# Fourier position transform with its 512-column moving operand turned afterwards, and query latents normed and turned ahead of it

## What is computed

```python
h = rmsnorm(x, ln_mix_g)
z = jnp.einsum('bsd,dn->bsn', h, w_in)
c_q, c_kv, k_rope, u = z[..., :o1], z[..., o1:o2], z[..., o2:o3], z[..., o3:]
y_mix = jnp.concatenate([mla(c_q, c_kv, k_rope, q_norm_g, w_uq, kv_norm_g, w_ukv),
                         fourier_mix(u, w_fnet)], axis=-1)
x = x + jnp.einsum('bsn,nd->bsd', y_mix, w_out)
...
def fourier_mix(u, w_fnet):
    B, S, _ = u.shape
    ug = u.reshape(B, S, FNET_GROUPS, FNET_GROUP_DIM).astype(jnp.float32)
    f = jnp.fft.fftn(ug, axes=(1, 3), norm='ortho').real.astype(u.dtype)
    return jnp.einsum('bsgc,gcd->bsgd', f, w_fnet).reshape(B, S, FNET_WIDTH)
```

## Time and profile before

| | us |
|---|---|
| median of 3 runs (lowest to highest) | 1427.01 (1426.34 to 1427.31) |
| the profiled execution | 1423.45 |
| its span, first to last instruction | 1421.7 |
| PE busy | 1381.4 (97%) |
| DVE / ACT / POOL busy | 810.4 / 656.9 / 834.7 |
| mean granted TensorE clock | 0.997 of full |

### The profile page before, as it was taken

One profiled execution on the slowest core, in us unless ns is written; L12 is line 12 of the kernel. 1 busy time (PEld: TensorE's weight loads), 2 busy tenths in 40 slices (PEclk: granted clock), 3 DMA queues, 4 the chain that ended last, 5 costly groups with the idle time before them and its releaser, 6 DMA issues. The chain is left out here.

```text
span 1421.7 us, 18322 instructions
## 1 busy us (share of the span) xinstructions
PE 1381.4 (97%) x6696; PEld 1159.3 (82%) x6696; DVE 810.4 (57%) x999; ACT 656.9 (46%) x1207; POOL 834.7 (59%) x631
## 2 busy tenths in 40 slices
PE   8999999999999999999999899999999999999998
PEld 6977779888889787888887688888888888878776
DVE  3576643134445574431645876666656664488966
ACT  5567635445335664553544533333323323444355
POOL 4648857741446677595246665555545554477884
PEclk9999999999999999999999999999999999999999
DMA  8401044513323101463144043332333325973234
GB/s 277 166 23 38 23 149 134 166 49 127 99 66 93 38 16 52 149 186 120 50 126 172 30 141 111 112 106 88 110 112 112 111 82 199 311 237 115 79 103 156
DMA packets 99145, 164.66 MB, mean 116 GB/s; under 512 B 8560, under 2 KB 40688, under 8 KB 99056
## 3 DMA queue, kind: packets, MB, share of 16 engines
q1 hardware_dynamic: 99056, 163.48, 35.1%
HBM read 134.88 MB, written 28.57 MB: 115 GB/s over the span
## 5 line engine op out<-in xcount | busy, mean ns | idle before, releaser
L749 POOL TENSOR_TENSOR w_lo<-w_raw,w_hi 128x512 fp32r<-128x512 f32 (+2 forms) x236 | 307.0, 1314 | 228.7 <-ACT w_hi L904 227.8
L1909 PE MATMUL ps<-h_hi_P,w_hi 128*128 128x512 f32 x616 | 241.2, 392 | 5.8 <-DVE h_lo_P L1350 3.1
L1910 PE MATMUL ps<-h_lo_P,w_hi 128*128 128x512 f32 x616 | 240.4, 390 | 0.0
L1911 PE MATMUL ps<-h_hi_P,w_lo 128*128 128x512 f32 x616 | 240.3, 390 | 0.0
L904 ACT ACTIVATE w_hi<-w_raw 128x512 fp32r<-128x512 f32 (+2 forms) x236 | 140.9, 608 | 197.0 <-PE ps L1911 180.8
L749 POOL TENSOR_TENSOR w_lo<-w_sum,w_hi 128x512 fp32r<-128x512 f32 x88 | 118.4, 1349 | 115.9 <-ACT w_hi L904 115.9
L749 POOL TENSOR_TENSOR w_lo<-a_raw,w_hi 128x512 fp32r<-128x512 f32 x77 | 111.9, 1455 | 74.2 <-ACT w_hi L904 74.1
L1909 PEld LDWEIGHTS ps<-h_hi_P,w_hi 128*128 128x128 f32 x616 | 116.0, 188 | 32.5 <-issue 4.7
L1909 PE MATMUL ps<-w_hi,act_hi 128*128 128x512 f32 (+2 forms) x384 | 140.6, 366 | 1.5 <-POOL w_lo L749 1.5
L1911 PE MATMUL ps<-w_hi,act_lo 128*128 128x512 f32 (+2 forms) x384 | 139.8, 364 | 0.0
L1910 PE MATMUL ps<-w_lo,act_hi 128*128 128x512 f32 (+2 forms) x384 | 139.8, 364 | 0.0
(11 more groups left out here) (242 smaller groups left out, 3046.1 us busy)
## 6 DMA issues: line engine op xcount, KB each, us to landing
gu_raw<-in_w_gate_up SPq DMA_DIRECT2D x22, 1024.0 KB, 5.5
a_raw<-a_mem SPq DMA_DIRECT2D x77, 256.0 KB, 2.7
w_raw<-in_w_xkv SPq DMA_DIRECT2D x64, 256.0 KB, 3.2
a_mem<-down_sum SPq DMA_DIRECT2D x44, 256.0 KB, 2.6
wd<-in_w_down SPq DMA_DIRECT2D x44, 256.0 KB, 5.6
a_mem<-act_t SPq DMA_DIRECT2D x33, 256.0 KB, 2.1
w_raw<-in_w_out SPq DMA_DIRECT2D x32, 256.0 KB, 2.6
w_raw<-in_w_xq SPq DMA_DIRECT2D x32, 256.0 KB, 2.9
```

The lines of the kernel that those rows point to most:

```text
L749: return nc.gpsimd.tensor_tensor(out, whole, hi.bitcast(F32), ALU.subtract)
L1909: nc.tensor.matmul(out, s_hi, m_hi, start=start, stop=False, skip_group_check=more)
L1910: nc.tensor.matmul(out, s_hi, m_lo, start=False, stop=False, skip_group_check=more)
L1911: return nc.tensor.matmul(out, s_lo, m_hi, start=False, stop=stop, skip_group_check=more)
```

## The change

The position transform takes the tables as the stationary operand and `f_hi`/`f_lo` moving, all four channel groups in one product of 512 columns (`fourier_class(k)`, four classes, each in a bank that z1 has left). Its output has positions on partitions. ACT copies it to a new `y_f`, and PE transposes it in 16 tiles (`fourier_positions(c)`) into the banks from which `fourier_out` goes on as before. PE's order becomes: `cq` transposes (3 x 4), four classes, `ck` transposes (2 x 4), `key_rope`, position transposes (4 x 4), query product. The query latents' squares and root (ACT) follow z0's scaling without the weight copies between, and their normed step (DVE) stands ahead of the second `fourier_in` pair. POOL rotates the key ahead of the two memsets, which now wait for the classes. DVE subtracts the latents ahead of the Fourier outputs. Some buffers change places, and banks and waits follow.

```diff
--- before.py
+++ after.py
@@ -133,7 +133,7 @@
...
              ("chan23", 4, None), ("z1", T, (w_in, KD, QR, ZW - QR)),
-             ("positions", FG, None), ("c", CQ + CK, None),
+             ("cq", CQ, None), ("ck", CK, None), ("positions", FG, None),
              ("vv", 16, (w_v, CK, 0, BANK)), ("kA", 0, (w_k, 1, 0, BANK)), ("q0", 0, (w_q, CQ, 0, BANK)),
@@ -234,22 +234,23 @@
...
         o1 = at("o1", R + 68, [P, 2, P])
+        y_f = at("y_f", R + 64, [P, ROOT, FG * P])
 
...
         c_gain = at("c_gain", R + 86.5, [P, QR + KR])
-        c_hi = at("c_hi", R + 44, [P, CQ + CK, S], F32R)
-        c_lo = at("c_lo", R + 54, [P, CQ + CK, S], F32R)
+        c_hi = at("c_hi", R + 6, [P, CQ + CK, S], F32R)
+        c_lo = at("c_lo", R + 16, [P, CQ + CK, S], F32R)
         k_rot = at("k_rot", R + 72, [P, 4, T, HALF])
...
         q_f = at("q_f", R + 4, [P, S])
-        v_hi_st = at("v_hi_st", R + 6, [P, T, PAIRS, 3, DV], F32R)
-        v_lo_st = at("v_lo_st", R + 18, [P, T, PAIRS, 3, DV], F32R)
+        v_hi_st = at("v_hi_st", R + 32, [P, T, PAIRS, 3, DV], F32R)
+        v_lo_st = at("v_lo_st", R + 44, [P, T, PAIRS, 3, DV], F32R)
         y_raw = at("y_raw", R + 30, [P, S])
-        kt_hi = at("kt_hi", R + 32, [P, 2, S], F32R)
-        kt_lo = at("kt_lo", R + 36, [P, 2, S], F32R)
-        prob = at("prob", R + 40, [P, 2, S])
+        kt_hi = at("kt_hi", R + 26, [P, 2, S], F32R)
+        kt_lo = at("kt_lo", R + 56, [P, 2, S], F32R)
+        prob = at("prob", R + 60, [P, 2, S])
         qt_hi = at("qt_hi", R + 64, [P, 2, S], F32R)
@@ -527,6 +530,7 @@
...
         FB = [TEN["positions"] + c for c in range(FG)]
+        FY_BANK = [(TEN["z1"] + k) % BANKS for k in range(ROOT)]
 
@@ -807,10 +811,10 @@
...
                     weights_lo(g, f"z{i}", 6, 8)
-                pool.wait_ge(psum_full.sem, psum_full.at(g, FA[FG - 1] + 2))
+                rotate_key(g)
+                pool.wait_ge(fy_full.sem, fy_full.at(g, ROOT))
                 nc.gpsimd.memset(v_hi_st[:, :, :, 1, :].bitcast(F32), 1.0).then_inc(v_filled.sem, 1)
                 nc.gpsimd.memset(v_lo_st[:, :, :, 1, :].bitcast(F32), 0.0).then_inc(v_filled.sem, 1)
-                rotate_key(g)
                 query_lo(g, 0)
@@ -1048,9 +1052,9 @@
...
                         for t in range(T):
-                            weights_hi(g, "z1", t, t + 1)
                             square(g, t, z[:, t, 0:QR], c_junk[:, 0:QR], T + t, QR)
                         root(g, T, T, T)
+                        weights_hi(g, "z1", 0, 4)
                     fourier_in(2 * i)
@@ -1060,10 +1064,15 @@
...
                 root(g, 2 * T, 0, T)
+                for f in range(CQ):
+                    hi_out(g, TEN["cq"] + f, c_hi[:, f, :], bank(TEN["cq"] + f))
+                for k in range(ROOT):
+                    act.wait_ge(fy_full.sem, fy_full.at(g, k + 1))
+                    copy(y_f[:, k, :], ps[:, FY_BANK[k], :]).then_inc(fy_copied.sem, 1)
+                for f in range(CK):
+                    hi_out(g, TEN["ck"] + f, c_hi[:, CQ + f, :], bank(TEN["ck"] + f))
                 for c in range(FG):
                     fourier_out(c)
-                for f in range(CQ + CK):
-                    hi_out(g, TEN["c"] + f, c_hi[:, f, :], bank(TEN["c"] + f))
                 key_rope_hi(g)
@@ -1514,12 +1523,6 @@
...
                     fourier_in(2 * i + 1)
-                    if i == 1:
-                        dve.wait_ge(cgain_in, (g + 1) * 32)
-                        invert(g, 0, T, T)
-                        for t in range(T):
-                            a = z[:, t, 0:QR]
-                            normed(a, a, T + t, c_gain[:, 0:QR]).then_inc(c_normed.sem, 1)
                     for t in range(T):
@@ -1528,17 +1531,23 @@
...
                                                 ALU.mult).then_inc(psum_free.sem, 1)
+                    if i == 0:
+                        dve.wait_ge(cgain_in, (g + 1) * 32)
+                        invert(g, 0, T, T)
+                        for t in range(T):
+                            a = z[:, t, 0:QR]
+                            normed(a, a, T + t, c_gain[:, 0:QR]).then_inc(c_normed.sem, 1)
 
...
                     normed(a, a, t, c_gain[:, QR:QR + KR]).then_inc(c_normed.sem, 1)
-                fourier_out(0)
-                fourier_out(1)
-                fourier_out(2)
-                fourier_out(3)
-                for f in range(CQ + CK):
-                    lo_out(g, HI["c"] + f, TEN["c"] + f, c_lo[:, f, :], bank(TEN["c"] + f), c_hi[:, f, :])
+                for f in range(CQ):
+                    lo_out(g, HI["cq"] + f, TEN["cq"] + f, c_lo[:, f, :], bank(TEN["cq"] + f), c_hi[:, f, :])
+                for f in range(CK):
+                    lo_out(g, HI["ck"] + f, TEN["ck"] + f, c_lo[:, CQ + f, :], bank(TEN["ck"] + f), c_hi[:, CQ + f, :])
+                for c in range(FG):
+                    fourier_out(c)
 
@@ -2000,7 +2009,7 @@
...
                 pe.wait_ge(krot.sem, krot.at(g, 12))
-                pe.wait_ge(psum_free.sem, psum_free.at(g, FB[1] + 1))
+                pe.wait_ge(psum_free.sem, psum_free.at(g, TEN["cq"] + 2))
                 for t in range(T):
@@ -2013,7 +2022,7 @@
...
                 if h == 0:
-                    pe.wait_ge(psum_free.sem, psum_free.at(g, TEN["c"] + k + 1))
+                    pe.wait_ge(psum_free.sem, psum_free.at(g, TEN["ck"] + CK if k == 0 else TEN["cq"] + k + 1))
                 o = slice(h % PAIRS * P, (h % PAIRS + 1) * P)
@@ -2027,7 +2036,7 @@
...
                 if p == 0:
-                    pe.wait_ge(psum_free.sem, psum_free.at(g, TEN["c"] + CQ + CK))
+                    pe.wait_ge(psum_free.sem, psum_free.at(g, TEN["ck"] + CK))
                 else:
@@ -2040,6 +2049,8 @@
...
                 pe.wait_ge(w_ready.sem, w_ready.at(g, w + 1))
+                if k == 0:
+                    pe.wait_ge(psum_free.sem, psum_free.at(g, FB[t] + 1))
                 o = slice(t * P, (t + 1) * P)
@@ -2054,7 +2065,7 @@
...
                     pe.wait_ge(kr_lo.sem, kr_lo.at(g, 2))
-                    pe.wait_ge(psum_free.sem, psum_free.at(g, FB[2] + 1))
+                    pe.wait_ge(psum_free.sem, psum_free.at(g, TEN["cq"] + 3))
                 if h > 0 or half > 0:
@@ -2133,18 +2144,26 @@
...
 
+                def fourier_class(k):
+                    pe.wait_ge(psum_free.sem, psum_free.at(g, TEN["z1"] + k + 1))
+                    out = ps[:, FY_BANK[k], :].rearrange("p (c d) -> p c d", c=FG)
+                    for a in range(2):
+                        last = three(out, dft_hi[:, a, k, :], dft_lo[:, a, k, :], f_hi[:, :, k, a, :], f_lo[:, :, k, a, :],
+                                     a == 0, a == 1)
+                    last.then_inc(fy_full.sem, 1)
+
                 def fourier_positions(c):
-                    pe.wait_ge(dft_ready, 1)
-                    pe.wait_ge(f_ready.sem, f_ready.at(g, c + 1))
-                    ten = FB[c]
-                    claim(g, ten)
-
-                    pe.wait_ge(psum_free.sem, psum_free.at(g, FA[c] + 1))
+                    claim(g, FB[c])
                     for k in range(ROOT):
-                        for a in range(2):
-                            last = three(ps[:, ten % BANKS, K1[k] * P:(K1[k] + 1) * P], f_hi[:, c, k, a, :],
-                                         f_lo[:, c, k, a, :], dft_hi[:, a, k, :], dft_lo[:, a, k, :],
-                                         a == 0, a == 1)
+                        last = nc.tensor.transpose(ps[:, FB[c] % BANKS, K1[k] * P:(K1[k] + 1) * P],
+                                                   y_f[:, k, c * P:(c + 1) * P], ident[:])
+                    last.then_inc(psum_full.sem, 1)
+
+                def latent(name, first, f):
+                    claim(g, TEN[name] + f)
+                    for t in range(T):
+                        last = nc.tensor.transpose(ps[:, (TEN[name] + f) % BANKS, t * P:(t + 1) * P],
+                                                   z[:, t, (first + f) * P:(first + f + 1) * P], ident[:])
                     last.then_inc(psum_full.sem, 1)
@@ -2152,16 +2171,18 @@
...
                                                               5: lambda: fourier_channels(3)})
-                for c in range(FG):
-                    fourier_positions(c)
-
+                pe.wait_ge(c_normed.sem, c_normed.at(g, T))
+                for f in range(CQ):
+                    latent("cq", 0, f)
+                pe.wait_ge(dft_ready, 1)
+                pe.wait_ge(f_ready.sem, f_ready.at(g, FG))
+                for k in range(ROOT):
+                    fourier_class(k)
                 pe.wait_ge(c_normed.sem, c_normed.at(g, 2 * T))
-                for f in range(CQ + CK):
-                    claim(g, TEN["c"] + f)
-                    for t in range(T):
-                        last = nc.tensor.transpose(ps[:, (TEN["c"] + f) % BANKS, t * P:(t + 1) * P],
-                                                   z[:, t, f * P:(f + 1) * P], ident[:])
```

(12 more changed lines are left out.)

## The result

| | before | changed |
|---|---|---|
| median of 4 runs, us | 1426.67 (1425.17 to 1427.31) | 1416.7 (1416.41 to 1417.6) |
| ratio | | 0.9935 [0.9918, 0.9951] |
| profiled execution, us (span) | 1423.45 (1421.7) | 1416.82 (1415.0) |
| end of z1 to the first `row_maxima`, group 0 (group 1), us | 21.33 (21.37) | 17.41 (17.41) |

A forecast was written before the change was run, and what follows sets the result against it. PE's instructions and waits were taken to bound the kernel. The stretch's terms summed to 17.26 us against 21.33, 4.07 less per group, 8.1 in both: 1415.3 profiled, plus 3.56 gives 1418.9 us, range 1416.0 to 1423.0.

The forecast's parts named there:

- 2. class 0: PE's four classes wait 0.92 us for POOL's last `f_lo`, start at 69.93, and take 5.44 us for 24 products.
- 3. key: After the `ck` transposes PE waits 0.38 us for POOL's twelve rotations, then transposes the rotary key until 77.10.
- 4. position transposes: PE's 16 position transposes take 1.79 us, to 78.89; ACT's copies stay hidden with 0.4 us cover.
- 5. query product: Query product to `row_maxima` takes 5.19 us, plus 0.85 us late because DVE's turned-bank copies, `q_f` and `kt_lo` queue.
- all later work is PE's, so I let all of it through: Behind the stage, the whole 4.07 us per group, 8.1 us in both, reaches the kernel's end.
- constant 3.56 us: The median lies 3.56 us above the profiled execution; added to the forecast 1415.3 us it gave 1418.9 us.
- Slower products: The 24 class products stream slower than 0.227 us each; at half speed 1429.8 us; chance 0.04.
- Full transposes: The 16 position transposes cost their full 0.27 us, not 0.112: 2.6 us less gained per group, 1424.1 us; chance 0.02.
- Upper bounds: PE's waits stay at their upper bounds, rotations at 77.85: 1421.3 us, or 1423.3 with later copies; chance 0.10.
- Waits vanish: PE's waits in the stage disappear: 6.2 us gained per group, 1414.6 us; chance 0.06.
- Nothing arrives: A later stage gives the gain back, so the kernel takes 1427 us; no change had chance 0.04.
- The clock falls: Behind transposes and waiting the clock drops to 1.2 GHz, doubling the 5.19 us after it: 1429 us; chance 0.02.

The follow-up runs named there:

- experiment 8: The kernel before, word for word, profiled a second time: 1426.82 us in the profiled execution.
- experiment 7: The kernel before plus eight unread 512-column products in PE's 1.9 us wait ahead of the query product: 1426.49 us, ratio 1.0003.
- experiment 12: The kernel before with eight unread 512-column products ahead of the query product and three more ahead of the latents' transposes: 1425.08 us, ratio 0.9997.
- experiment 2: The changed kernel without the early squares and normed step, `cq` transposes and copies moved behind the classes: 1431.5 us, ratio 1.0031.
- 1: The kernel before with only the query latents' squares, root and normed step moved early, position products kept: 1419.47 us, ratio 0.994.
- 3: The changed kernel with PE's wait for POOL's last `f_lo` moved from ahead of class 0 to ahead of class 2: 1415.88 us, ratio 0.992.
- 4: The changed kernel with the `f_lo` wait behind two classes and POOL's key rotation ahead of z1's last two weight subtractions: 1416.73 us, ratio 0.9922.
- 5: The changed kernel with DVE and ACT copying position banks 0 and 1, then the rotary key (DVE also `q_f`), then banks 2 and 3: 1414.21 us, ratio 0.9918.
- 6: The changed kernel with reordered DVE and ACT copies, the `f_lo` wait behind two classes and earlier key rotation: 1412.31 us, ratio 0.9904.
- experiment 9: The changed kernel, word for word, measured again against the kernel before: 1416.13 us, ratio 0.993.
- 10: The changed kernel with reordered DVE and ACT copies, later `f_lo` wait and earlier key rotation, measured a second time: 1413.21 us, ratio 0.9907.
- 11: The kernel before with only the early squares, root and normed step, measured a second time: 1420.04 us, ratio 0.9952.

## Why the prediction was right, and where its sizes were off

**The path, by the prediction's steps.** Group 0, predicted and measured:

| step | predicted | measured |
|---|---|---|
| 1. `cq` transposes; cover behind the normed step | 67.67; 1 us | 67.68; 0.67 us |
| 2. class 0, and the wait ahead of it | 69.93, 0.92 | 69.93, 0.94 |
| 2. the 24 products | 5.44 | 5.57 |
| 3. key, and the wait ahead of it | 76.65, 0.38 | 76.49, 0.12 |
| 4. position transposes | 77.10, 1.79 | 76.98, 1.67 |
| 5. query product; `q_f` begins | 78.89; 82.7 | 78.65; 82.71 |
| 5. `kt_lo` done; `row_maxima`, and its wait | 84.85; 84.93, 0.85 | 84.83; 85.08, 1.55 |
| gain of the stretch | 4.07 | 3.92 |

The waits are counted here as the prediction counts them, from where PE's next product could have started; the view counts from the modelled end of the last one and shows 0.78, nothing and 1.39. Every wait named in the forecast is where it was put. What the last one waits for, DVE's `kt_lo`, is done at the time named to 0.02 us, and `row_maxima` starts 0.15 later than forecast. The wait is 0.7 larger than forecast: the 5.19 us from query product to `row_maxima` contained 0.3 us of waits of their own (the bare work is 4.88), the query product came 0.24 earlier, and 0.15 comes behind `kt_lo`. PE arrives earlier and waits longer, for nearly the same end. The key's wait is 0.12 where 0.38 was put: POOL's twelve rotations took 4.15 us, from 72.28, and PE came 0.13 later. The unknown cost, four runs of 128 elements as the moving operand, is next to nothing: the first product takes 0.30 and the 23 others 0.229 each, where six products of the projection took 0.227. The ACT cover in step 4 was 0.35 us (0.4 forecast).

**Step "all later work is PE's, so I let all of it through" failed by 1.2 us.** PE's lead over the first profile of before is 3.93 us behind group 0's stage and 3.45 at 201 us: group 0's waits on DVE's `m_tok` have grown from 1.6 to 2.1, as DVE has as much to do as ever (811.2 us busy against 810.4) and PE reaches it sooner. In group 1 the lead grows from 3.4 to 7.37, and is 6.98 at the next query product (the wait on `q_f` went from 0.38 to 0.65) and 6.6 at the end. So 7.88 us come in at the two stretches and 6.6 arrive.

**The constant 3.56 us between the profile and the median was the larger error, with the other sign.** I added it to the changed kernel, whose profiled execution (1416.82) lies at its own median (1416.7). So the profiled execution was forecast 1.5 us too low (1415.3) and the step to the median 3.7 too high, and the smaller error hid part of the larger: that the median lies in the range, 0.7 us above its lower end, is partly luck. The 3.56 were no constant: experiment 8, a second profile of before, took 3.37 us longer than the first, and its two stretches are 3.58 longer (23.70 + 22.58 against 21.33 + 21.37); that the two figures lie so close is in part chance, since the first profile has a clock spell at 810 us that the second lacks. The median of before holds disturbances in the very stage that the change rebuilds, and the first profile happened to have none. There are two:

1. *DVE's normed step against POOL's subtraction.* Which of the two is slowed varies; when DVE is, PE comes 1.1 us later. In the four profiles of kernels with the old order (before, 7, 8, 12), DVE lost in 3 of 8 groups. It goes by a hundredth of a microsecond: POOL's subtraction starts 0.023, 0.028 and 0.033 us behind DVE's second step in the three groups that DVE lost, and 0.037 to 0.043 behind it in the five others and in both groups of experiment 2, where POOL was the one slowed. With the normed step at 56.24 it meets weight subtractions instead, takes 4.35 or 4.36 in all 18 groups of nine profiles (the changed kernel and experiments 1, 3 to 6 and 9 to 11), and has 0.67 us of cover. The prediction priced this meeting at POOL's 0.42 us and wrote beside it that a full lock could cost more; the case where DVE pays was not looked for.
2. *The clock.* In 3 of those 8 groups the granted clock fell to 1.2 GHz for about 3.4 us: twice among the query products, behind the 128-column products, the transposes and both waits (experiment 8), once among the transposes, behind the 128-column products and a wait of 1.63 (experiment 7). Two of the three are groups in which DVE had lost. In 14 groups of the new order (the changed kernel, experiments 3, 4, 5, 6, 9 and 10) and 4 groups of experiments 1 and 11 it didn't fall there. Elsewhere it falls in either order: the first profile of before has such a spell at 809.8 us and that of the changed kernel at 802.7, while the second profile of each has none there; of all fourteen profiles ten have one or two, near 200 or near 800 us. So they are no sign of the old order as such, only of this stage in it. The mean clock of the timed runs agrees: 0.9954 to 0.9959 before, 0.9973 and 0.9976 changed, and 0.0015 to 0.002 of 1425 us is 2 to 3 us, an estimate that experiment 12 doesn't bear out: the same rise gave 0.5 us there.

Over its two profiles the stretch of before averages 22.25 us, against 17.40: 4.85 a group, 9.7 in both, and less the 1.2 given back 8.5, where 9.3 (7.0 to 11.7) and in experiment 9 10.0 (8.1 to 12.0) were measured. Two profiles are few for such a mean.

What is shown of this: the gain of the stretch, what a second execution adds, and that both disturbances are absent from this stage in all 18 groups of the new order. What makes the clock fall in before is **open**. Filling one wait (7) or two (12) gave no time back; in 7 the fall came ahead of the fill, and in 12 none came in the stage and the clock's mean did rise, but a single profile cannot say how the rest was lost. The narrow products alone do not bring the clock down, nor do they with the 24 transposes behind them, as far as four groups can tell: experiments 1 and 11 keep both, and it stayed at 1.00 there. Whether it is the length of the waits was not separated from their place.

**The rivals.** *Slower products* falls by the pitch of 0.229. *Full transposes* falls: 16 in 1.67 us, the 0.27 being the last one's latency, so the lower of the two prices was right. What the Trainium skill (TensorE: Matmul & The Clock Gate, "Part 4: PE-mode transpose") gives for one transpose, about 275 ns, is met as latency only. *Upper bounds* falls: the key waited 0.12. *Waits vanish* falls: 2.6 us of waits were left (2.2 by the view), and experiments 5 and 6 show that it takes DVE's order to remove them. *Nothing arrives* falls. *The clock falls* did not happen in the changed kernel; it did in experiment 2, after a wait of 5.32, for 2.9 and 2.0 us instead of the 5.2 I had put on it, and it happened in the kernel before, where I had not looked since the first profile read 1.00.

## What to carry to other kernels

Before adding the parts of a change, ask which part frees the buffers that the other one writes: here either part alone gave 2.2 us or a loss, and both 3.9. When PE's work shrinks, read the next engine's serial list from the point where PE will arrive; its order, not its length, was worth another 1.3 us per group at `row_maxima` and 0.8 at the first scores (experiment 5). And a profiled execution below the median is a hint that the median holds something: take a second profile and compare stage by stage before that difference is treated as a constant.

## What was not expected of the hardware

- **DVE and POOL take turns by whole instructions, and who waits changes from run to run.** DVE's four normed steps taken one by one, in the first and the second profile of before, group 0 (columns: count, shortest/median/longest ns, first and last start):

```profile
L1369 DVE SCALAR_TENSOR_TENSOR z<-z,stats,c_gain x4: 606/1146/1635, 68.3 to 71.0; 128x384 f32<-128x384 f32 x4
```

```profile
L1369 DVE SCALAR_TENSOR_TENSOR z<-z,stats,c_gain x4: 678/1630/1724, 67.6 to 71.4; 128x384 f32<-128x384 f32 x4
```

A step next to nothing takes some 0.6 us and one that waits for a POOL subtraction of 1.29 takes 1.6. A median of 1146, the mean of the middle two, says two short and two long; one of 1630 says three long. One more turn lost is the 1.1 us. The Trainium skill (SBUF — State Buffer, "SBUF: two separate sides") states that whichever of the two starts first gets the shared ports for its whole instruction; steps of two lengths agree with that, and would not come from a steady sharing. Who gets them can't be read from the recorded starts alone: DVE's second step starts first in all ten groups, and still waits in the three in which its lead is 0.033 us or less.
- **The clock falls for some 3.4 us in a kernel whose PE is busy for 97%**, in this stage in 3 of 8 groups and at 810 us in one profile of two, with the code the same; and in every group in which PE had stood still for 5.3 us (experiment 2, both, for 6.8 us).
- **A moving operand in four runs of 128 fp32r elements costs PE next to nothing**: 0.229 us per product against 0.227 in one run. Where ACT and DVE write with a step of four elements, they take longer: four `act_hi` 3.91 us against five `c_hi` 2.58, and four `act_lo` 4.13 against five `c_lo` 3.14.
